# Attention stages: who copies the second head's turned weights, and which copy each wait names

## The reference, cut to what matters

```python
s_loc = jnp.einsum('bnqhgd,bnkhd->bnhgqk', qb, kb).astype(jnp.float32) * scale
s_loc = jnp.where(ok[None, :, None, None], s_loc, -jnp.inf)
s_ctx = jnp.einsum('bnqhgd,bchd->bnhgqc', qb, kc).astype(jnp.float32) * scale
p = jax.nn.softmax(jnp.concatenate([s_sink, s_ctx, s_loc], axis=-1), axis=-1)
...
o = jnp.einsum('bnhgqc,bchd->bnqhgd', p_ctx, vc) + jnp.einsum('bnhgqk,bnkhd->bnqhgd', p_loc, vb)
```

## Time and profile before

| | |
|---|---|
| median of 3 executions | 2973.07 us (2971.12 to 2974.59) |
| profiled execution | 2971.06 us, of which the span of its instructions 2969.0 us |
| busy PE / DVE / ACT | 2715.1 / 2015.8 / 1533.8 us |
| mean granted PE clock | 0.955 of full speed |
| first attention | from 172 to 275 us of the span |
| causal attentions | from 1418 to 1480 us and from 2697 to 2752 us |

### The profile page before, as it was taken

How to read it: one execution, slowest core, us unless ns; L and a number is a source line. 1 busy time by engine, 2 the same in 40 slices (tenths; PEclk the granted TensorE clock), 3 DMA queues, 4 the chain that set the end, 5 groups by cost and what they waited for, 6 DMA issues and landing times. The chain is left out here.

```text
span 2969.0 us, 55869 instructions
## 1 busy us (share of the span) xinstructions
PE 2715.1 (91%) x21466; PEld 2454.4 (83%) x21466; DVE 2015.8 (68%) x3472; ACT 1533.8 (52%) x2626; POOL 107.0 (4%) x132
## 2 busy tenths in 40 slices
PE   7997989996797999879799998999988899998999
PEld 4855579995656999869699988999888799996999
DVE  2157478895474999767467775677865577785677
ACT  3256367884553888644643354434742343446443
POOL 1010001110000111000000000000000000000000
PEclk9999989997897999979899999999989999999999
DMA  8292179996362999934045542455530155542453
GB/s 291 86 290 66 57 240 362 359 360 238 112 200 87 352 357 356 338 94 132 30 154 172 170 124 91 163 177 170 161 128 1 43 170 171 165 133 72 150 186 118
DMA packets 421328, 528.96 MB, mean 178 GB/s; under 512 B 14288, under 2 KB 387328, under 8 KB 420496
## 3 DMA queue, kind: packets, MB, share of 16 engines
q1 hardware_dynamic: 408480, 499.72, 50.9%
q0 software_dynamic: 9216, 12.61, 1.3%
q10 hardware_dynamic: 3440, 13.98, 1.3%
HBM read 526.16 MB, written 21.06 MB: 184 GB/s over the span
## 5 line engine op out<-in xcount | busy, mean ns | idle before, releaser
L2065 DVE TENSOR_TENSOR W_lo<-ring,W_hi 128x1024 fp32r<-128x1024 f32 x384 | 452.8, 1222 | 60.1 <-ACT W_hi L1982 58.6
L2250 PE MATMUL ps<-H_part,W_hi 128*128 128x272 f32 (+2 forms) x1800 | 416.5, 306 | 25.3 <-DVE H_part L2154 12.7
L1982 ACT ACTIVATE W_hi<-ring 128x1024 fp32r<-128x1024 f32 x384 | 385.0, 1053 | 69.2 <-DMA ring<-in_w_up 23.1
L2783 ACT ACTIVATE W_hi<-ring 128x1024 fp32r<-128x1024 f32 x264 | 263.1, 1049 | 294.0 <-PE ps L2756 185.3
L2734 PE MATMUL ps<-room_part,W_hi 128*128 128x272 f32 (+1 forms) x1408 | 404.4, 287 | 5.0 <-DVE room_part L2154 5.0
L2735 PE MATMUL ps<-room_part,W_hi 128*128 128x272 f32 (+1 forms) x1408 | 403.6, 287 | 0.0
L2736 PE MATMUL ps<-room_part,W_lo 128*128 128x272 f32 (+1 forms) x1408 | 402.8, 286 | 0.0
L2250 PEld LDWEIGHTS ps<-H_part,W_hi 128*128 128x128 f32 x1800 | 303.1, 192 | 43.6 <-issue 28.8
L2823 DVE TENSOR_TENSOR W_lo<-ring,W_hi 128x1024 fp32r<-128x1024 f32 x264 | 314.1, 1219 | 10.3 <-ACT W_hi L2783 9.4
L2250 PE MATMUL ps<-H_part,W_lo 128*128 128x272 f32 (+2 forms) x1024 | 305.2, 298 | 0.0
L1895 PE MATMUL ps<-W_hi,A_split_hi 128*128 128x256 f32 x1024 | 294.0, 287 | 7.7 <-DVE A_split_lo L2071 7.7
(11 more groups left out here) (505 smaller groups left out, 5898.3 us busy)
## 6 DMA issues: line engine op xcount, KB each, us to landing
ring<-in_w_down SPq DMA_DIRECT2D x108, 1024.0 KB, 7.1
ring<-in_w_gate_up SPq DMA_DIRECT2D x88, 1024.0 KB, 5.1
ring<-in_w_gate SPq DMA_DIRECT2D x64, 1024.0 KB, 9.0
ring<-in_w_up SPq DMA_DIRECT2D x64, 1024.0 KB, 9.1
ring<-in_w_mod SPq DMA_DIRECT2D x48, 1024.0 KB, 6.5
ring<-in_fox_w_in SPq DMA_DIRECT2D x32, 1024.0 KB, 5.7
ring<-in_gdn_w_in SPq DMA_DIRECT2D x16, 1024.0 KB, 5.5
ring<-in_gla_w_in SPq DMA_DIRECT2D x12, 1024.0 KB, 5.2
```

The lines of the kernel that those rows point to most:

```text
L1982: act.activation(self.parts(p)[0][:, W], c.ring[:, g % SLOTS, W], ACT.Copy).then_inc(c.hi_done, 1)
L2065: dve.tensor_tensor(lo, c.ring[:, (self.g0 + p) % SLOTS, W], hi.bitcast(F32), ALU.subtract)\
L2250: mm = pe.matmul(self.out(i), a, b, start=(k == 0 and n_part == 0), stop=(k == KC - 1 and n_part == 2))
L2783: act.activation(self.slot_parts(p)[0][:, C], c.ring[:, g % SLOTS, C], ACT.Copy).then_inc(c.hi_done, 1)
```

## The change

In the first attention, for each pair, the copy of the second head's bank is made by DVE (`second_vector`), behind the maximum and the weights of the same step; ACT keeps the copy of the first head's bank. In all attentions each copy now sets a mark of its own, `("turned", i, u)`. The turning into bank u waits for the copy of bank u alone, and the product with the values waits for all the copies of its item. The two causal attentions keep both copies on ACT (`SECOND_ON_VECTOR` is False there).

```diff
@@ Attention.tensor
                     if self.user(i, u) is not None:
-                        pe.wait_ge(self.scalar_done, self.act.at("turned", self.user(i, u)))
+                        pe.wait_ge(*self.copied_out(self.user(i, u), u))
...
             for i in self.due(step, 3):
                 it = self.items[i]
-                pe.wait_ge(self.scalar_done, self.act.at("turned", i))
+                for u in self.buffers[i]:
+                    pe.wait_ge(*self.copied_out(i, u))
...
+    SECOND_ON_VECTOR = False
+
+    def by_vector(self, i, u):
+
+        return self.SECOND_ON_VECTOR and self.pair(i) and u == 1
+
+    def copied_out(self, i, u):
+        return (self.vector_done, self.dve.at("turned", i, u)) if self.by_vector(i, u) else (self.scalar_done, self.act.at("turned", i, u))
+
+    def second_vector(self, dve, step):
+        for i in self.due(step, 2):
+            for u in self.buffers[i]:
+                if self.by_vector(i, u):
+                    w = len(self.blocks(self.items[i])) * P
+                    dve.wait_ge(self.tensor_done, self.pe.at("turned", i, u))
+                    if self.user(i, u) is not None:
+                        dve.wait_ge(self.tensor_done, self.pe.at("out", self.user(i, u)))
+                    dve.tensor_copy(self.pT[:, u, 0:w], self.c.ps[:, 4 + u, 0:w]).then_inc(self.vector_done, self.dve.mark("turned", i, u))
@@ Attention.vector
                 ins.then_inc(self.vector_done, self.dve.mark("weights", i, 0))
+            self.second_vector(dve, step)
             if self.follow:
                 self.ahead_vector(dve, step)
-        if self.follow:
-            for step in range(self.steps_through(1), N + 6 + self.lag()):
+        for step in range(self.steps_through(1), max(self.steps_through(2), N + 6 + self.lag())):
+            self.second_vector(dve, step)
+            if self.follow and step < N + 6 + self.lag():
                 self.ahead_vector(dve, step)
@@ Attention.scalar
                 for u in self.buffers[i]:
+                    if self.by_vector(i, u):
+                        continue
                     act.wait_ge(self.tensor_done, self.pe.at("turned", i, u))
                     if self.user(i, u) is not None:
                         act.wait_ge(self.tensor_done, self.pe.at("out", self.user(i, u)))
-                    ins = act.activation(self.pT[:, u, 0:w], c.ps[:, 4 + u, 0:w], ACT.Copy)
-                ins.then_inc(self.scalar_done, self.act.mark("turned", i))
+                    act.activation(self.pT[:, u, 0:w], c.ps[:, 4 + u, 0:w], ACT.Copy).then_inc(self.scalar_done, self.act.mark("turned", i, u))
@@ WindowAttention
+    SECOND_ON_VECTOR = True
```

## The result

The changed kernel takes 2958.04 us (median of 5 runs, 2957.2 to 2961.81) against 2973.14 us for the kernel before beside it (5 runs, 2971.12 to 2974.59): ratio 0.995, 95% interval 0.9938 to 0.9962. A second set of runs gave -11.9 us (plus or minus 3.2; 5 runs against 21), so 12 to 15 us is the size. Its profiled execution took 2958.04 us, span 2956.2.

A forecast was written before the change was run, and what follows sets the result against it. First attention bound by PE, then by a ring of waiting engines, then by DVE. Terms 2.5 + 2.0 + 2.3 = 6.8 us, so 2973.07 becomes 2966.3 us; 8 in 10 range 2963.0 to 2972.8.

The forecast's parts named there:

- First attention, 2.5 us: Whole first attention: 0.4 us from its PE bound steps 0 to 12 plus 2.1 us kept from steps 14 to 19.
- the ring: First attention, steps 14 to 19: turning, exponentials, copies, turning wait for each other, 3.78 us a round; shortened by 2.44 us.
- step 4: First attention, PE bound part: the turning there waits for the copies and would start 0.28 us earlier.
- the last turning: End of the first attention's pair steps: the turning of item 16 would start 2.35 us earlier than at 241.23 us.
- the DVE bound stretch: First attention's differential heads, 241 to 275 us, DVE busy 30.82 of 34 us: would keep 2.1 us of the gain.
- 1.85 and 0.30: Start of the differential heads: DVE's chain ahead by 1.85 us plus a 0.30 us wait for PE that goes, 2.15 us.
- DVE has room, 0 us: First attention: the added DVE copies hide in gaps where DVE waits for PE, 1.63 us in step 15; no loss.
- Nothing downstream absorbs it: Behind the attentions: the loads stand still with the weights' ring full, so the whole 6.8 us reaches the end.
- What follows moves as a whole: Stages behind the gain: loads restart when PE frees a slot, so everything later shifts by the same amount.
- The causal attentions, 4.3 us: Both causal attentions: each turning waits for its own copy alone, 2.0 us in the earlier and 2.3 in the later.
- more than forecast: Rival, chance 0.10: a drop of the granted clock falls away, 1.6 us, plus upper causal bounds; -10.3 us, 2962.8 us.

The follow-up runs named there:

- e1: Changed kernel with the finer waits alone, both copies left on ACT in all attentions, against the kernel before: 0.9964, -12.5 us.
- c4: Changed kernel with each DVE copy of the first attention made twice, against the kernel before: 0.9962, -12.2 us.
- c3: Kernel before with four chained squares added on ACT behind the first attention as a delay, against the kernel before: 1.0011, +3.6 us.
- g4: First attention as changed, causal ones with joint waits, plus four chained squares behind the first attention, against the kernel before: 0.9990, -2.8 us.
- f2: Finer waits in the causal attentions alone, first attention as before, against the kernel before: 0.9967, -9.0 us.
- e2: Second copies moved to DVE in the first attention, joint waits kept everywhere, against the kernel before: 0.9979, -6.5 us.
- e3: First attention as changed, causal attentions with the joint waits of before, against the kernel before: 0.9980, -6.6 us.
- g3: The kernel of e3 run again, against the kernel before: 0.9976, -6.7 us.
- h1: Kernel before with 31 one-column memsets added on DVE at 33 us, where it idles, against the kernel before: 0.9983, -4.6 us.
- f1: Kernel before with seven turnings added on PE in each of the last four steps of both causal attentions, against the kernel before: 0.9981, -6.1 us.
- f3: Changed kernel with seven turnings added on PE in each of the last four steps of both causal attentions, against the kernel before: 0.9952, -13.9 us.
- f4: Second copies on DVE and finer waits in all attentions, plus the added PE turnings, against the kernel before: 2952.89 us, 0.9935, -19.2 us.
- g1: Kernel before with seven PE turnings added in each of the last four steps of the later causal attention alone: 0.9992, -2.7 us.

## Why the prediction was wrong

By its own steps:

- **First attention, 2.5 us: right.** Measured 2.6 us to the end of the ring and 2.4 to the end of the stage, in the places named: step 4 gives 0.30 (0.28 forecast), the ring's steps 0.5, 0.5, 0.2, 0.3, 0.5 and 0.5 us (0.47 or 0.28 each), the last turning 2.48 us ahead (2.35), the DVE bound stretch keeps 2.1 of the ring's gain (2.1). Of the last figure's parts, 1.85 and 0.30, the 1.85 us stands in the prediction without a working, so that its total came out is in part luck. The split was wrong: the moved copy was taken to be what brings the gain, and the finer wait alone brings 2.0 us (e1). The working looked at copies that end earlier, not at a turning whose first half needs only the first of them; it did so only for the causal attentions.
- **DVE has room, 0 us: right.** It is used up in the ring when the copies double (c4: 1.9 us, against 2.5 to 3.7 expected).
- **Nothing downstream absorbs it: right as far as it went** (c3, g4: 3.4 us of delay costs 3.6 and 3.8 us, with errors of 2 and 3). "What follows moves as a whole" left out that a program which is 31 instructions longer on DVE meets its branch at another place: 3.1 us, a term that is missing from the sum.
- **The causal attentions, 4.3 us: the step that failed.** The term counted the waits alone, and the stages gave 9.3: 3.5 us for the earlier (3.8 on the mean of five executions with the finer wait, 3.3 to 5.5, less 0.3 on the mean of nine without), 5.8 for the later (6.2 on the mean, 5.5 to 6.8, less 0.5). The wait's part was well sized where it can be read undisturbed: 2698 to 2744 us gains 2.65 us in e1, c4 and f2, where 2.3 were forecast; in the changed kernel itself 1.4, since the short drop of the clock at 2725.7 us falls into it. What was left out of the forecast is what hangs on it: the drop of the granted clock at the end, 4.1 us in the later attention. The prediction had this as the rival "more than forecast", with a tenth of the chance, and priced it with 1.6 us from the first stretch. The row that prices it was there to be read: a window over the tail shows a granted clock of 0.65 for 12 us, so 0.35 x 12 = 4.2 us lost. The rows read for the prediction have the clock of the first attention alone.

The sum by stages, each at its end, is 2.4 + 3.1 + 3.5 + 5.8 = 14.8 us, against 15.1 and 11.9 measured. The same four terms give the other kernels (us; the finer waits alone 2.0 in the first attention, the moved copies alone 2.6, c4 1.9 less, g4 3.4 less):

```
                       terms                      sum   measured (2 errors)
e1 finer waits only    2.0 + 3.5 + 5.8           11.3   12.5 (2.9)
e2 moved copies only   2.6 + 3.1                  5.7    6.5 (1.9)
e3, g3 first only      2.4 + 3.1                  5.5    6.6 (1.6), 6.7 (1.9)
g4 first only, delayed 2.4 + 3.1 - 3.4            2.1    2.8 (2.2)
f2 causal only         3.5 + 5.8                  9.3    9.0 (2.1)
c4 copies twice        2.4 + 3.1 + 3.5 + 5.8 - 1.9  12.9   12.2 (3.0)
h1 longer program      3.1                        3.1    4.6 (2.5)
```

All lie within their errors. The kernels with added turnings do not add up so well: the same reckoning from their one profile each gives 8.9 us for f1, 17.2 for f3 and 23.2 for f4, against 6.1, 13.9 and 19.2 measured (errors 1.8, 1.5 and 1.5). Why they keep less than their stages show stays open. How the 3.5 us of the earlier causal attention divide into waits and clock stays open: its drops lie at other places in each execution. So does what makes the clock fall later or not at all; the runs show that more PE work in the tail keeps it up, and that the late drop was absent wherever the finer wait was.

## What to carry to other kernels

Before pricing a wait near the end of a stage, read the granted clock behind it: where it falls in the tail, a fraction of a us a step, or added work on an idle PE, can decide over 4 us here. Where the program branches, compare the time from the branch to the engine's next instruction between kernels of different length; a change that adds or removes instructions ahead of it can move that time by 3 us, for reasons that have nothing to do with the edit, and a few memsets where the engine idles can buy it. Count the packets of instructions ahead of the branch as well as behind it: a window that ends when the engine goes on hides those that come later. When a gain is larger than its parts, subtract the starts of the same instructions and look for the neighbours between which the gain jumps.

## What the runs showed of the hardware

- Behind a branch DVE needs either 1.44 to 1.47 us or 3.9 to 4.6 us until its next instruction, and the place of the branch in its program decides: 1.44 to 1.45 us in all twelve executions whose target stands 796 or 812 instructions from the start of the program as it is built, 1.47 with 1572; 4.0 to 4.6 in all eight with 765, 3.9 to 4.4 in all nineteen with 1491, 1522 or 1538. A packet of instructions on q14 9.5 to 16.7 us ahead of the branch goes with each short wait and with no long one. ACT, with the same branch, took 0.40 to 0.44 us in all.
- Waiting for each of two copies by itself was worth nearly as much as moving one of them to another engine (2.0 and 2.6 us; both together 2.4).
- Work added to an idle TensorE made the kernel faster: 56 turnings, 6.1 us plus or minus 1.8 (f1). The granted clock of the later tail was then 1.00 instead of 0.65 (g1).
- One kernel's executions differ by up to 7 us between 300 and 1310 us, nearly all of its spread; with 11 and 31 runs a difference of means is known to 2 us (g1).
